# The causal mask of prompt attention: added by VectorE in PSUM in place of a bf16 product on TensorE

## Chip, cores and metric

The kernel runs on one core of one Trainium2 chip. The metric is device time in microseconds for one execution, lower is better. TensorE does matrix products and transposes into PSUM, VectorE and ScalarE read PSUM, GpSimd works on SBUF only, SyncE issues most of the DMAs.

## The reference

One step of a hybrid decoder layer: latent attention and a Mamba-2 scan in parallel, a gated merge, layer norm and a SwiGLU network, for a prompt of 1024 tokens and for 8 sequences with 4 new tokens each. Only the attention of the prompt matters here. Per head, of 16:

```python
def block(i):                       # 128 queries
    s = (einsum('bqhd,bkhd->bhqk', qn, k_nope)
         + einsum('bqhr,bkr->bhqk', qp, k_pe)).astype(float32) * ATTN_SCALE
    mask = key_pos[None, :] <= q_pos[:, None]
    s = where(mask, s, finfo(float32).min)
    p = softmax(s, axis=-1).astype(v.dtype)
    return einsum('bhqk,bkhd->bqhd', p, v)
```

A block of 128 queries with number q sees the (q + 1) * 128 keys up to its own end. Only the last 128 of these, the diagonal block, are cut by the mask.

## The kernel before

Each engine runs its own instruction list, written by hand, and semaphores order them. A stage of projections and of the scan comes first, then the prompt's attention (1218 to about 1530 us of the trace), then attention over the cached pages, then the branch products and the feed-forward network.

Attention handles two heads at a time, eight pairs in all. A pair's eight blocks of queries are split: G = 1 are the later four (q = 7 to 4, scores of 1024 to 640 keys), G = 0 the earlier four (q = 3 to 0, 512 to 128 keys). In each group the index i runs from 0 to 7: i % 2 is the head, i // 2 counts the blocks down from the longest. So there are 16 rows of scores in a pair, 128 in all.

PSUM has eight banks of 512 fp32. Head 0's scores are in banks 0 and 1, head 1's in banks 2 and 3. A row of G = 1 takes both banks of its head; rows of G = 0 take one, in turn. Bank 4 holds turned probabilities of head 0, bank 5 those of head 1, banks 6 and 7 the outputs.

For one row:

- TensorE (`scores`, L1155) multiplies the queries by the keys, 96 deep, in pieces of up to 512 keys. The product is fp32, and the trace shows two instructions for each piece. It waits for `s_read0` or `s_read1`, by which ScalarE says that the banks have been read.
- TensorE (L1157) adds the mask to the diagonal block: a bf16 identity `ident_b` times a bf16 table `after_b`, which holds 0 where a key is allowed and -1e30 where not. This product signals `s_ready`.
- VectorE (`row_max`, L2154) takes the row maximum from PSUM and scales it by a constant (L2156), which signals `m_ready`.
- ScalarE (`probs`, L1668) does the exponential with that maximum as bias, into SBUF (`pr`), with the row's sum beside it, and signals `s_read`.
- VectorE (`row_inverse`, L2161) takes the reciprocal of the sum of the row before; GpSimd (`scale_probs`, L805) multiplies the probabilities by it.
- TensorE turns the probabilities in tiles of 128x128 (`turn_probs`, L1169), head 0 then head 1. VectorE copies head 0's to SBUF (`turned`, L2166, `pt_read0`) and ScalarE head 1's (L1674). The next `turn_probs` waits for those copies.
- TensorE multiplies them by the values (`weigh`, L1179); ScalarE copies a finished output (`head_out`, L1679) and stores it.

The order on TensorE interleaves two groups. `later_rows` does the scores of G = 1 and turns and weighs the probabilities of G = 0; `earlier_rows` does the scores of G = 0 of the next pair and turns and weighs G = 1 of this one. VectorE's and ScalarE's lists follow the same order. Eight rows of G = 0 of the first pair stand ahead of all that. The inner pairs are a loop of two.

The tables `ident_b` and `after_b` are made by two casts on VectorE (L2133, L2134) at the end of the stage before; TensorE waits for them (`bf_ready`).

Of the kernel before, what the change touches and what calls it, by code (L numbers as in the profile page):

```python
# [9 lines left out]
BF16 = mybir.dt.bfloat16  # L10
I32 = mybir.dt.int32
ALU = mybir.AluOpType
# [3 lines left out]
P = 128  # L16
# [4 lines left out]
HEADS, NOPE, ROPE, VH = 16, 64, 32, 64  # L21
# [60 lines left out]
@contextmanager  # L82
def looped(eng, count, per):

    begun = {t: t.n for t in per}
    with eng.Fori(0, count) as i:
        for t, p in per.items():
            t.loops.append((i, p, t.n))
        yield i
    wrong = {t.sem.name: t.n - begun[t] for t, p in per.items() if t.n - begun[t] != p}  # L90
    assert not wrong, wrong
    for t, p in per.items():
        t.loops.pop()
        t.n += p * (count - 1)
# [57 lines left out]
def build(nc, a, o, stop=99, debug=None):  # L152
# [21 lines left out]
    def sem(name):  # L174
        if name in taken:
            return sem(taken[name][0])
        if name not in sems:
            sems[name] = nc.alloc_semaphore(name)
        return sems[name]
# [52 lines left out]
    def const(name):  # L232
        at, n = where[name]
        return cst[:, at:at + n]

    ident, ones = const("ident"), const("ones")
    V_GATE, V_QN, V_KVN, V_SSM, V_L1G, V_L1B, V_L2G, V_L2B, V_END = 0, 16, 19, 21, 37, 45, 53, 61, 69

    ps = nc.alloc_psum_tensor("ps", [P, 8, 512], F32)
# [30 lines left out]
    ar = Arena(floor)  # L270
# [5 lines left out]
    ar = Arena(floor)  # L276
# [20 lines left out]
    ar = Arena(floor)  # L297
# [9 lines left out]
    ar = Arena(at_conv)  # L307
# [24 lines left out]
    ar = Arena(at_z)  # L332
# [7 lines left out]
    ar = Arena(at_st)  # L340
# [3 lines left out]
    ar = Arena(at_cw)  # L344
# [3 lines left out]
    ar = Arena(at_cv)  # L348
# [3 lines left out]
    ar = Arena(at_so)  # L352
    s_new = [ar(f"s_new{b}", [P, 4, P]) for b in range(NEWS)]
    assert ar.at <= at_ccol
    ar = Arena(at_ccol)
    s_xe[1] = ar("s_xe1", [P, HG, SP_])
    assert ar.at <= at_crow
    ar = Arena(at_crow)
# [4 lines left out]
    ar = Arena(at_xo)  # L363
# [5 lines left out]
    ar = Arena(low)  # L369
# [24 lines left out]
    ar = Arena(at_kvt)  # L394
# [3 lines left out]
    ar = Arena(at_kvt)  # L398
    olat = ar("olat", [P, 2, HEADS, NS])
    oats = ar("oats", [P, HEADS // 2, NS])  # L400
    qb, kb, vb = [], [], []
    ar = Arena(low)
    for pp in range(2):
        qb.append([ar(f"qb{pp}{h}", [QH, SEQ]) for h in range(2)])
        kb.append([ar(f"kb{pp}{h}", [QH, SEQ]) for h in range(2)])
        if pp == 1:
            assert ar.at <= at_wkv
            ar = Arena(at_kvt)
        vb.append([ar(f"vb{pp}{h}", [P, SEQ // P, VH]) for h in range(2)])
    ident_b, after_b = ar("ident_b", [P, P], BF16), ar("after_b", [P, P], BF16)  # L410
    assert ar.at <= floor
    ar = Arena(at_g)
    pr = [[ar(f"pr{G}{i}", [P, (4 * G + 4 - i // 2) * P]) for i in range(8)] for G in range(2)]
# [5 lines left out]
    ar = Arena(low)  # L419
# [8 lines left out]
    ar = Arena(low)  # L428
# [399 lines left out]
    def _(pe):  # L828
        k = Counts()
        pe.wait_ge(sem("ident_full"), 16)  # L830

        for t in range(9):
# [4 lines left out]
            for j in range(KT):  # L837
                at = ps[:, 2 * b + j // 4, (j % 4) * n:(j % 4) * n + n] if n == P else ps[:, 2 * b, j * n:j * n + n]
# [161 lines left out]
        for j in range(DI // P):  # L1000
            last = pe.matmul(ps[:, 6, j * NS:(j + 1) * NS], spread[0:SH, j * P:(j + 1) * P], act_[:, SEQ:TOK],
                             start=True, stop=True)
# [137 lines left out]
            pe.wait_ge(sem(f"third_free{c}"), k[f"third_free{c}"].next())  # L1140
        pe.wait_ge(sem("xd_ready"), k["xd_ready"].next())
        pe.wait_ge(sem("kr_full"), k["kr_full"].next(64))
        pe.wait_ge(sem("bf_ready"), k["bf_ready"].next(2))

        def scores(pp, G, i):

            q, h, b = 4 * G + 3 - i // 2, i % 2, i % 2
            if G == 0 and i == 0:
                pe.wait_ge(sem(f"head_full{pp}"), k[f"head_full{pp}"].next(96))
            first_bank = 2 * b + (i // 2 % 2 if G == 0 else 0)  # L1150
            pe.wait_ge(sem(f"s_read{b}"), k[f"s_read{b}"].held() - (1 if G == 0 and i >= 2 else 0))
            length = (q + 1) * P
            for c in range(0, length, 512):
                w = min(512, length - c)
                pe.matmul(ps[:, first_bank + c // 512, 0:w], qb[pp][h][:, q * P:(q + 1) * P], kb[pp][h][:, c:c + w], start=True, stop=True)  # L1155
            at = q * P
            last = pe.matmul(ps[:, first_bank + at // 512, at % 512:at % 512 + P], ident_b[:, :], after_b[:, :], start=False, stop=True,  # L1157
                             skip_group_check=True)
            last.then_inc(sem("s_ready"), k["s_ready"].adds(1))

        def turn_probs(G, kb_):
# [689 lines left out]
    def _(dve):  # L1851
        k = Counts()
# [277 lines left out]

        dve.wait_ge(sem("unit_done"), 74)
        dve.tensor_copy(ident_b[:, :], ident).then_inc(sem("bf_ready"), k["bf_ready"].adds(1))  # L2133
        dve.tensor_copy(after_b[:, :], const("after")).then_inc(sem("bf_ready"), k["bf_ready"].adds(1))  # L2134

        def page_rows():
            dve.memset(krs[:, :], 0.0).then_inc(sem("pads_ready"), k["pads_ready"].adds(1))
# [10 lines left out]
        def row_max(G, i):  # L2148
            n = G * 8 + i
            length = (4 * G + 4 - i // 2) * P  # L2150
            first_bank = 2 * (i % 2) + (i // 2 % 2 if G == 0 else 0)
            src = ps[:, first_bank:first_bank + 2, :].rearrange("p a n -> p (a n)")[:, 0:length] if G else ps[:, first_bank, 0:length]
            dve.wait_ge(sem("s_ready"), k["s_ready"].next())
            dve.tensor_reduce(rowmax[:, n:n + 1], src, AX, ALU.max).then_inc(step.sem, step.adds(1))  # L2154
            dve.wait_ge(step.sem, step.same())
            dve.tensor_scalar(negmax[:, n:n + 1], rowmax[:, n:n + 1], -SCALE, None, ALU.mult).then_inc(sem("m_ready"), k["m_ready"].adds(1))  # L2156
# [29 lines left out]
                row_inverse(0, i - 1)  # L2186
        later_rows()
        page_rows()
        with looped(dve, HEADS // 4 - 1, {k["s_ready"]: 32, step: 32, k["m_ready"]: 32, k["inv_ready"]: 32, k["t_ready0"]: 24,
                                          k["pt_read0"]: 24} | pairs(k, {"s_read": 16})):  # L2190
            earlier_rows()
            later_rows()
            earlier_rows()
            later_rows()
# [313 lines left out]
```

## Time and profile before

| | us |
|---|---|
| median of 3 runs | 3173.14 |
| lowest and highest run | 3171.33, 3176.74 |
| profiled execution | 3172.03 |
| its span | 3170.2 |
| one pair of heads, from its first long score row to the next pair's | 37.45 |

The profile counts an engine as busy from an instruction's start to its end. A TensorE product's end is modelled and lies after the last column has gone in, so the ends of products overlap the next ones. What a product costs TensorE is read from start to start. Times within the trace count from the span's start.

### The profile page before, as it was taken

How to read it: one execution, taken by the hardware profiler on the slowest of the kernel's cores; microseconds unless marked ns; L12 is line 12 of the kernel's file. 1: busy time of each engine (PE TensorE's matmuls, PEld its weight loads, DVE VectorE, ACT ScalarE, POOL GpSimd, SP SyncE). 2: the span in 40 equal slices, each digit the busy share in tenths (PEclk: the TensorE clock that was granted, in tenths of full speed). 3: DMA queues.
4: the chain of work that ended last, by engine and by line, in shares of the span. 5: the costliest groups of instructions: out<-in, count | busy, mean ns of one | idle time of the engine just before them, and what ended most of it. 6: DMA issues, size and time to landing. Idle time of an engine off the chain costs nothing.

```text
span 3170.2 us, 46396 instructions
## 1 busy us (share of the span) xinstructions
PE 2978.9 (94%) x19012; PEld 2626.6 (83%) x19012; DVE 1558.7 (49%) x2120; ACT 756.7 (24%) x1151; POOL 1016.8 (32%) x546
## 2 busy tenths in 40 slices
PE   7889999999999999999999978999889999999996
PEld 7767999989998995555677668899789999999995
DVE  1661677774746464555344467665352222222226
ACT  1111121253535353545323110100120000000003
POOL 3331333332323322444211113344323333433330
PEclk9999999999999997999899989999999999999997
DMA  4134223555746445222343323353201111111101
GB/s 131 39 112 125 83 82 117 153 148 143 178 135 177 139 121 151 60 60 69 130 179 141 111 92 108 103 170 115 61 31 44 47 40 46 40 46 40 46 20 55
DMA packets 313405, 308.22 MB, mean 97 GB/s; under 512 B 31094, under 2 KB 271995, under 8 KB 310779
## 3 DMA queue, kind: packets, MB, share of 16 engines
q1 hardware_dynamic: 249768, 190.26, 21.3%
q10 hardware_dynamic: 59914, 78.22, 7.4%
q0 software_dynamic: 3584, 37.75, 3.1%
q8 instruction: 105, 1.72, 0.2%
q14 instruction: 34, 0.27, 0.0%
HBM read 227.97 MB, written 78.20 MB: 97 GB/s over the span
## 4 chain that ended last, share of the span: by engine, by line
PE 68%; DVE 12%; issue 9%; POOL 4%; DMA 3%; ACT 2%; SPq 1%; ACTq 0%; POOLq 0%; DVEq 0%
PE ps L859 41%; PE ps L1025 10%; POOL pr L805 4%; PE ps L1358 2%; PE ps L1301 2%; PE ps L1261 2%; PE ps L1274 2%; DVE cv L1956 2%; DVE flo L2445 1%; PE ps L1278 1%; PE ps L933 1%; PE ps L1104 1%; DVE cv L1950 1%; PE ps L1058 1%; DMA gt<-d_z 1%
## 5 line engine op out<-in xcount | busy, mean ns | idle before, releaser
L737 POOL TENSOR_TENSOR whi<-raw,cst 128x1024 fp32r<-128x1024 f32 x172 | 334.0, 1942 | 1404.9 <-PE ps L859 1273.1
L739 POOL TENSOR_TENSOR wlo<-raw,whi 128x1024 fp32r<-128x1024 f32 x172 | 469.5, 2730 | 13.5
L859 PE MATMUL ps<-ahi,whi 128*128 128x352 f32 x1824 | 400.2, 328 | 51.7 <-DVE alo L2316 21.5
L859 PE MATMUL ps<-alo,whi 128*128 128x352 f32 x1824 | 398.2, 327 | 0.0
L859 PE MATMUL ps<-ahi,wlo 128*128 128x352 f32 x1824 | 395.0, 325 | 0.0
L859 PEld LDWEIGHTS ps<-ahi,whi 128*128 128x128 f32 x1824 | 313.5, 191 | 58.7 <-issue 34.5
L859 PEld LDWEIGHTS ps<-ahi,wlo 128*128 128x128 f32 x1824 | 314.9, 190 | 0.0
L859 PEld LDWEIGHTS ps<-alo,whi 128*128 128x128 f32 x1824 | 313.6, 189 | 0.0
L1025 PE MATMUL ps<-xhi,whi 128*128 128x352 f32 x768 | 257.3, 335 | 0.6 <-ACT xraw L1534 0.4
L1025 PE MATMUL ps<-xlo,whi 128*128 128x352 f32 x768 | 248.8, 324 | 0.0
L1025 PE MATMUL ps<-xhi,wlo 128*128 128x352 f32 x768 | 248.8, 324 | 0.0
L2343 DVE TENSOR_TENSOR mm<-ps,mm 128x1056 f32<-128x1056 f32 x112 | 139.6, 1256 | 147.7 <-PE ps L859 146.3
L805 POOL TENSOR_TENSOR pr<-pr,rowinv 128x384 f32<-128x384 f32 (+7 forms) x128 | 145.5, 1146 | 202.5 <-DVE rowinv L2161 201.5
L1155 PE MATMUL ps<-kb,qb 96*128 96x512 f32 (+3 forms) x384 | 161.2, 538 | 10.8 <-ACT pr L1668 8.3
L859 PE MATMUL ps<-xhi,whi 128*128 128x352 f32 x720 | 158.4, 328 | 6.5 <-ACT xraw L1534 4.3
L859 PE MATMUL ps<-xlo,whi 128*128 128x352 f32 x720 | 157.3, 327 | 0.0
L859 PE MATMUL ps<-xhi,wlo 128*128 128x352 f32 x720 | 156.6, 326 | 0.0
L2154 DVE TENSOR_REDUCE rowmax<-ps 128x1 f32<-128x384 f32 (+7 forms) x128 | 96.9, 757 | 118.1 <-PE ps L1157 116.4
L1025 PEld LDWEIGHTS ps<-xhi,whi 128*128 128x128 f32 x768 | 145.3, 189 | 9.2 <-issue 6.8
L1155 PEld LDWEIGHTS ps<-kb,qb 96*128 96x128 f32 x384 | 65.5, 198 | 105.4 <-issue 76.9
L1025 PEld LDWEIGHTS ps<-xlo,whi 128*128 128x128 f32 x768 | 145.4, 189 | 0.0
L1025 PEld LDWEIGHTS ps<-xhi,wlo 128*128 128x128 f32 x768 | 145.2, 189 | 0.0
(320 smaller groups left out, 5015.8 us busy)
## 6 DMA issues: line engine op xcount, KB each, us to landing
raw<-in_w_in SPq DMA_DIRECT2D x61, 512.0 KB, 5.0
s_a<-d_acum SPq DMA_DIRECT2D x32, 512.0 KB, 7.1
d_xbc<-so ACTq DMA_DIRECT2D x24, 528.0 KB, 2.7
gt<-d_g SPq DMA_DIRECT2D x24, 528.0 KB, 3.7
raw<-in_w_ffn_gate SPq DMA_DIRECT2D x22, 512.0 KB, 3.7
raw<-in_w_ffn_up SPq DMA_DIRECT2D x22, 512.0 KB, 3.7
raw<-in_w_ffn_down SPq DMA_DIRECT2D x22, 512.0 KB, 3.5
d_z<-zo ACTq DMA_DIRECT2D x16, 528.0 KB, 5.0
```

Of the source, the lines that this page charges most:

```text
L737: pool.tensor_tensor(whi[s][:, :], raw[:, u], ones[:, 0:1].broadcast_to([P, UNIT]), ALU.mult).then_inc(sem("unit_hi"), k["unit_hi"].adds(1))
L739: pool.tensor_tensor(wlo[s][:, :], raw[:, u], whi[s][:, :].bitcast(F32), ALU.subtract).then_inc(sem("unit_split"), k["unit_split"].adds(1))
L805: pool.tensor_tensor(pr[G][i][:, :], pr[G][i][:, :], rowinv[:, n:n + 1].broadcast_to([P, length]), ALU.mult).then_inc(sem("n_ready"), k["n ...
L859: last = pe.matmul(ps[0:m, 3 * b + c, 0:width], w(j), x[:, j, at:at + width], start=i == 0, stop=i == n - 1)
L1025: last = pe.matmul(ps[:, c, 0:CH], w[u % SPLIT][:, j * P:(j + 1) * P], x[:, j, c * CH:(c + 1) * CH], start=i == 0, stop=i == 3 * KT - 1)
L1155: pe.matmul(ps[:, first_bank + c // 512, 0:w], qb[pp][h][:, q * P:(q + 1) * P], kb[pp][h][:, c:c + w], start=True, stop=True)
L1261: last = pe.transpose(ps[:, 4 + i % 3, r * P:(r + 1) * P], src, ident)
L1274: pe.matmul(half(c, s), qcur[b][:, j, :], kvt[:, j, 4 * g:4 * g + 4, :].rearrange("p r n -> p (r n)"), start=j == 0, stop=False)
L1301: last = pe.matmul(ps[64 * s:64 * s + 64, 7, 0:KL], prt[:, i, 64 * s:64 * s + 64], kvb[b][:, 8 * c + 4 * s + i % 4, :], start=i == 0, stop ...
L1358: last = pe.matmul(ps[:, 3 * b + c, 0:width], ones, src[:, at:at + width], start=start, stop=stop_)
L2154: dve.tensor_reduce(rowmax[:, n:n + 1], src, AX, ALU.max).then_inc(step.sem, step.adds(1))
L2343: dve.tensor_tensor(thirds(mm[:, e]), out3(b), thirds(mm[:, e]), ALU.add).then_inc(sem(f"res_free{b}"), k[f"res_free{b}"].adds(1))
```

## The change

The product L1157 goes, and so do the two bf16 tables, their casts and the wait for them. `s_ready` is now signalled by the last piece of the scores. VectorE gets a new first step in `row_max`: it adds the fp32 table `after`, which lies in SBUF already, to the diagonal 128 columns of the scores, reading and writing the same place in PSUM. The row maximum waits for this addition, on VectorE's own semaphore `dve_step`. The table in fp32 has the same values as the bf16 one.

```diff
-    ident_b, after_b = ar("ident_b", [P, P], BF16), ar("after_b", [P, P], BF16)
...
-        pe.wait_ge(sem("bf_ready"), k["bf_ready"].next(2))
...
                 w = min(512, length - c)
-                pe.matmul(ps[:, first_bank + c // 512, 0:w], qb[pp][h][:, q * P:(q + 1) * P], kb[pp][h][:, c:c + w], start=True, stop=True)
-            at = q * P
-            last = pe.matmul(ps[:, first_bank + at // 512, at % 512:at % 512 + P], ident_b[:, :], after_b[:, :], start=False, stop=True,
-                             skip_group_check=True)
+                last = pe.matmul(ps[:, first_bank + c // 512, 0:w], qb[pp][h][:, q * P:(q + 1) * P], kb[pp][h][:, c:c + w], start=True, stop=True)
             last.then_inc(sem("s_ready"), k["s_ready"].adds(1))
...
         dve.wait_ge(sem("unit_done"), 74)
-        dve.tensor_copy(ident_b[:, :], ident).then_inc(sem("bf_ready"), k["bf_ready"].adds(1))
-        dve.tensor_copy(after_b[:, :], const("after")).then_inc(sem("bf_ready"), k["bf_ready"].adds(1))
...
             dve.wait_ge(sem("s_ready"), k["s_ready"].next())
+            own = src[:, length - P:length]
+            dve.tensor_tensor(own, own, const("after"), ALU.add).then_inc(step.sem, step.adds(1))
+            dve.wait_ge(step.sem, step.same())
             dve.tensor_reduce(rowmax[:, n:n + 1], src, AX, ALU.max).then_inc(step.sem, step.adds(1))
...
-        with looped(dve, HEADS // 4 - 1, {k["s_ready"]: 32, step: 32, k["m_ready"]: 32, k["inv_ready"]: 32, k["t_ready0"]: 24,
+        with looped(dve, HEADS // 4 - 1, {k["s_ready"]: 32, step: 64, k["m_ready"]: 32, k["inv_ready"]: 32, k["t_ready0"]: 24,
```

No other instruction moves. VectorE's list shows it best in the earlier rows at i = 0 and 1, E0 and E1 in the prediction (`t_ready0` says that head 0's turned probabilities are in PSUM, `s_read` that a row's exponential is done). Before:

```order
L2154 TENSOR_REDUCE rowmax<-ps 128x1 [waits s_ready]
L2156 TENSOR_SCALAR negmax<-rowmax 128x1 [waits dve_step]
L2161 RECIPROCAL rowinv<-rowsum 128x1 [waits s_read1]
L2166 COPY ptb_213<-ps 128x128 [waits t_ready0]
L2154 TENSOR_REDUCE rowmax<-ps 128x1 [waits s_ready]
L2156 TENSOR_SCALAR negmax<-rowmax 128x1 [waits dve_step]
L2161 RECIPROCAL rowinv<-rowsum 128x1 [waits s_read0]
L2166 COPY ptb_211<-ps 128x256 [waits t_ready0]
```

With the change, the same place (the buffers' numbers differ, the buffers do not):

```order
L2151 TENSOR_REDUCE rowmax<-ps 128x1 [waits dve_step]
L2153 TENSOR_SCALAR negmax<-rowmax 128x1 [waits dve_step]
L2158 RECIPROCAL rowinv<-rowsum 128x1 [waits s_read1]
L2163 COPY ptb_211<-ps 128x128 [waits t_ready0]
L2149 TENSOR_TENSOR ps<-ps,cst 128x128 [waits s_ready]
L2151 TENSOR_REDUCE rowmax<-ps 128x1 [waits dve_step]
L2153 TENSOR_SCALAR negmax<-rowmax 128x1 [waits dve_step]
L2158 RECIPROCAL rowinv<-rowsum 128x1 [waits s_read0]
L2163 COPY ptb_209<-ps 128x256 [waits t_ready0]
```

The addition stands right behind the wait for the scores, ahead of the reciprocal and of the copy of the same step. Nothing changes places otherwise.

## Rows read from the trace of the kernel before

**Rows 1.** The page: busy time of the engines, share of the span, instructions
```profile
PE 2978.9 (94%) x19012; PEld 2626.6 (83%) x19012; DVE 1558.7 (49%) x2120; ACT 756.7 (24%) x1151; POOL 1016.8 (32%) x546
```

**Rows 2.** Busy time by stretches: stretch, length, busy us per engine, clock, DMA
```profile
1218.00:1240.00 22.00, 18.56 (x39) 8.74 (x40) 8.05 (x28) 7.44 (x20) 5.50 (x8) 0.54 0.56 169
...
1296.00:1332.00 36.00, 35.32 (x177) 18.28 (x175) 20.77 (x57) 17.79 (x43) 17.37 (x16) 1.00 0.20 59
```

**Rows 3.** The score line's products: min/median/max ns, first and last start, forms
```profile
L1155 PE MATMUL ps<-kb,qb x384: 272/592/1192, 1217.9 to 1515.1; 96*128 96x512 f32 x96, 96*128 96x384 f32 x32, 96*128 96x256 f32 x32, 96*128 96x128 f32 x32
```

**Rows 4.** Timeline: start us, us, engine, operation, count, idle before in brackets
```profile
1302.83 0.22 PE L1157 MATMUL ps<-after_b,ident_b 128*128 128x128 bf16 x1
...
1302.89 1.04 PE L1169 MATMUL ps<-cst,pr 128*128 128x128 f32 x8
1303.09 0.42 DVE L2154 TENSOR_REDUCE rowmax<-ps 128x1 f32<-128x256 f32 x1 [1.31 <-PE ps L1157]
1303.55 0.15 DVE L2156 TENSOR_SCALAR negmax<-rowmax 128x1 f32<-128x1 f32 x1
...
1309.60 1.98 PE L1155 MATMUL ps<-kb,qb 96*128 96x512 f32 x4
...
1347.05 1.98 PE L1155 MATMUL ps<-kb,qb 96*128 96x512 f32 x4
```

**Rows 5.** Timeline of rows L1 to L4 of the same pair
```profile
1314.14 0.19 ACT L1668 ACTIVATION_READ_ACCUMULATOR pr<-ps,negmax 128x1 f32 x1
...
1314.63 0.19 PEld L1155 LDWEIGHTS ps<-kb,qb 96*128 96x128 f32 x1 [0.33 <-ACT pr L1668]
...
1314.68 1.72 PE L1155 MATMUL ps<-kb,qb 96*128 96x512 f32 x4
...
1317.59 1.77 PE L1155 MATMUL ps<-kb,qb 96*128 96x512 f32 x4 [0.31 <-ACT pr L1668]
...
1318.63 1.01 ACT L1668 ACTIVATE pr<-ps,negmax 128x896 f32<-128x896 f32 x1 [0.60 <-ACT att L1679]
...
1319.78 1.56 PE L1155 MATMUL ps<-kb,qb 96*128 96x512 f32 x4 [0.36 <-ACT pr L1668]
```

**Rows 6.** Timeline of L6, E1 and E2 of that pair
```profile
1323.41 0.19 ACT L1668 ACTIVATION_READ_ACCUMULATOR pr<-ps,negmax 128x1 f32 x1
...
1324.02 1.30 PE L1155 MATMUL ps<-kb,qb 96*128 96x512 f32 x4
...
1330.16 0.19 ACT L1668 ACTIVATION_READ_ACCUMULATOR pr<-ps,negmax 128x1 f32 x1
...
1330.52 1.12 PE L1155 MATMUL ps<-kb,qb 96*128 96x512 f32 x2
...
1332.68 0.42 DVE L2166 COPY ptb<-ps 128x256 f32<-128x256 f32 x1
...
1333.20 0.42 PEld L1169 LDWEIGHTS ps<-cst,pr 128*128 128x128 f32 x4 [0.22 <-DVE ptb L2166]
...
1333.26 0.82 PE L1169 MATMUL ps<-cst,pr 128*128 128x128 f32 x6
```

**Rows 7.** Groups of VectorE: additions, or products, that read PSUM
```profile
L2097 DVE SCALAR_TENSOR_TENSOR s_new<-s_in,cdp,ps 128x128 f32<-128x128 f32 x128 | 35.9, 342 | 118.7 <-PE ps L1104 118.7
...
L2042 DVE TENSOR_TENSOR s_cb<-ps,cst 128x128 f32<-128x128 f32 x32 | 9.3, 289 | 46.9 <-ACT s_bt L1599 46.9
...
L2233 DVE TENSOR_TENSOR snew<-ps,cst 64x32 f32<-64x32 f32 x8 | 1.4, 172 | 0.0
```

**Rows 8.** Timeline of the start of the stage
```profile
1217.92 2.04 PE L1155 MATMUL ps<-kb,qb 96*128 96x512 f32 x2 [2.42 <-DVE after_b L2134]
...
1225.78 1.28 ACT L1668 ACT_TABLE_LOAD   x1 [15.00 <-DMA d_y<-s_y]
...
1231.66 0.27 DVE L2154 TENSOR_REDUCE rowmax<-ps 128x1 f32<-128x128 f32 x1
...
1232.10 3.75 PE L1155 MATMUL ps<-kb,qb 96*128 96x512 f32 x4 [0.52 <-ACT pr L1668]
```

## The prediction

> **What bounds the kernel now.** I read the page first. TensorE is busy for 94% of the span and VectorE for 49% [rows 1], so time taken from TensorE should count and time given to VectorE should be hidden. That is an average over stages, and the change touches one stage only: prompt attention, from 1218 to about 1530 us. The busy time by stretches says the same of it: TensorE 35.3 of 36 us, VectorE 20.8 of 36, clock 1.00 [rows 2]. So I went on to the order of events. VectorE's row maximum stood idle 1.31 us for the mask product at 1303.09 [rows 4]: VectorE, and ScalarE after it, hang on the product's end, with little queued before it. Last I read TensorE's own waits for softmax, in the timeline, for they tell whether a longer VectorE step is hidden.
>
> One pair of heads takes 37.45 us from its first score row to that of the next pair, 1309.60 to 1347.05 [rows 4]. There are eight pairs. I call the score rows of a pair L0 to L7 (rows of 1024 to 640 keys) and E0 to E7 (512 to 128 keys, of the next pair). Even numbers use one pair of banks, odd ones the other, so a score row waits until ScalarE's exponential of the row two before has read its banks. In this pair TensorE is already late at two rows: L3 starts 0.31 us and L4 0.36 us after TensorE fell idle, both released by the exponential [rows 5].
>
> **What is removed.** 128 mask products, 16 in a pair. The 0.22 us shown for one is not its price: TensorE is pipelined. The product starts at 1302.83 and the next transpose at 1302.89, so one costs 0.06 us of TensorE; the weight load lies under the row before [rows 4]. That is 0.96 us a pair and 7.7 us in all, if each counted. The end of a row is also signalled earlier, by 0.06 us: the product's start plus 0.22, against the last score product's stream end (the same moment) plus the 0.16 that a score product of 128 keys takes beyond its stream. That 0.16 is 0.27 us, the shortest score product, less 0.11 us, the step from one transpose of 128 columns to the next (eight take 1.04 us, the last 0.27 of it) [rows 3, 4].
> The two VectorE casts that made the bf16 tables go too. TensorE waited for the second until 1217.92, but ScalarE does its first exponential only after 1227.06, behind a wait for stores and a table load of 1.28 us [rows 8]; the first four rows fill the banks and then stand still for that. The 2.4 us so saved lie in this wait: worth nothing.
>
> **What is added.** 128 VectorE additions of 128x128 fp32, from PSUM and a constant into the same PSUM, plus a wait of the row maximum for it. No row of this trace has VectorE writing PSUM. The nearest row, PSUM and the constant table into SBUF at 128x128, is 289 ns. Below it stands a smaller one, 64x32, at 172; above it one with a third operand at 342 [rows 7]. I take 0.29 and keep 0.17 and 0.40 (the 342 with a margin of 60 ns for an unseen destination) as ends. The hand-over from one VectorE step to a dependent one is 0.035 us (row maximum from 1303.09 for 0.42, its scaling at 1303.55) [rows 4]. So each row's exponential comes 0.29 + 0.035 - 0.06 = 0.27 us later, counted from the end of its scores. On VectorE's queue the addition also stands ahead of the reciprocal for the row before and of the copy of turned probabilities.
> The Trainium skill (VectorE: DVE Perf Modes, The TRN2 errata) gives (N+151)/0.96 ns for an fp32 tensor_tensor, which is 291 ns here; its table of fixed costs gives 120 + N cycles from PSUM, 258 ns, by which the estimate would be about 1.2 us lower. The row's 289 ns agrees with the first. Its rules for authors say to minimise the count of chained VectorE operations, not the semaphores, which speaks against this change.
>
> **What of it is on the path, in one pair.** I go along TensorE and keep the lag behind the old schedule.
> - L0 and L1 run on without a wait. L1 starts 0.06 early.
> - L2 waits for L0's exponential. That was read out by 1314.33 and L2's weight load came at 1314.63. With 0.27 more and 0.05 for the semaphore the load comes at 1314.65 and the product 0.11 later, 1314.76 in place of 1314.68: lag 0.08.
> - L3 was already held by L1's exponential. L1 was 0.06 early and its exponential is 0.27 later: lag 0.21.
> - L4 is held through ScalarE's queue (a copy of the head's output and its store stand before L2's exponential): lag still 0.21 [rows 5].
> - L5 starts at 0.15. L6 waits for L4's exponential, read out by 1323.60, against a start at 1324.02. Add 0.21 and 0.27: 1324.08, plus 0.05 for the semaphore and 0.11 for the load, is 1324.24: lag 0.22.
> - E0 has no wait in this trace; the masks of L6 and L7 gone, the lag falls to about 0.1. E1 waits for L7's exponential, read out by 1330.35 (the read after it starts at 1330.16 and takes 0.19), against 1330.52. It gets L7's lag of 0.15 plus 0.27, so 1330.82 with the semaphore: lag 0.3 [rows 6].
> - E2's transposes wait for VectorE's copy at E1. It ended at 1333.10 and the transposes started at 1333.26: no slack, since 0.05 and 0.11 lie between. The copy now stands behind E1's addition: 0.3 + 0.27: lag 0.57 [rows 6]. The row of the weight load at 1333.20 names this copy as what ended its idle time.
> - From there nothing waits; the five masks of E3 to E7 give back 0.30.
> So a pair ends 0.27 us later, with about 1.5 us of new or longer waiting and 0.96 of product gone, less what the old waits swallowed. Seven such pairs: 1.9 us. Four additions of the 16 stand in the chain.
>
> **The start.** Before the first pair, eight rows of short scores run at clock 0.54 [rows 2], and the tail of it is VectorE and ScalarE turn by turn: the last maximum starts at 1231.66, each waiting behind the reciprocal of the row before, then L0 at 1232.10 when the seventh row's is out [rows 8]. Five additions (third to seventh row), 5 x 0.325 = 1.6, less 0.2 where ScalarE and not VectorE set the pace: 1.4 us, with no TensorE time to give back. The first long rows at half clock: 0.3. The last pair reaches L7's addition, whose exponential frees the gather of cached pages: 0.1 us. Sum: 1.4 + 1.9 + 0.3 + 0.1 = 3.7 us.
> The profiled execution takes 3172.03 us, 1.8 more than its span and 1.1 less than the median of 3173.14. I put the 3.7 on the median: **3176.8 us**, 0.12% slower, which is within 0.2% (6.3 us), about what a measurement of this kernel can tell from no change.
>
> **Its bounds.** In the sum, 0.01 us of addition is worth 28 x 0.01 in the pairs and about 9 x 0.01 at the start and the end, 0.37 us. An addition of 0.17 gives -0.7 us, 0.22 no change, 0.34 gives +5.5, 0.36 the mark of 6.3, 0.40 gives +7.8. The clock is still low in the first stretch; if it rises 3 us earlier or later than before, that moves about 1 us. With the spread of the three runs, 5.4 us, this makes 3171 to 3184.
>
> **Rivals.**
> 1. *The addition into PSUM is dear* (slower by over 0.2%). Reading and writing PSUM in one operation has no row. From 0.36 us on the time passes the mark; at 0.45 the four chained additions cost 0.9 us a pair and the total is about +9.6: 3182.7. For it: no row shows the destination, and the three-operand row has 342. Against: the fixed parts of the copy, maximum and addition rows from PSUM lie close together. 0.23.
> 2. *The products were free already.* If the next fp32 load only moves into the place of the mask's hidden load, the 0.06 isn't given back and the pair ends 0.8 us later in all, not 0.27: 7 x 0.8 + 1.8 = 7.4, 3180.5. Against: transposes with the same kind of load follow each other at 0.11 us, just their streaming [rows 4]. 0.05.
> 3. *VectorE hides it all* (faster). The chain at L3, E1 and E2 would have to have slack; then 0.96 a pair comes back less 1.4 at the start: -5.3, and at most -7.7: 3165.4 to 3167.8. For it: VectorE idles 15 us of 36. Against: the three waits above. Faster by over the mark: 0.05.
> 4. *The clock.* New waits of 0.3 us lower the granted clock once a pair: taken as 3 us at half speed, 1.5 us lost, eight times: +12 on top, 3189. The Trainium skill (TensorE: Matmul & The Clock Gate, Part 1) ties the clock to recent activity. In this stage the clock stays at 1.00 with waits of 0.3 to 0.4 us present [rows 2, 5]. 0.02.
> My own case has 0.65.
>
> **Chances.** Some of my case's upper end and rival 2 pass the mark, some of rival 3 stays below it: faster 0.05, within 0.2% 0.66, slower 0.29.
>
> **What would show it.** The addition's row near 290 ns, 128 times; the pair's period up by about 0.27 from 37.45; TensorE's wait at E1 and at E2's transposes new, about 0.3 each; L3's idle time 0.2 longer and L4's unchanged; L0 of the first pair 1.4 us later; transposes starting 0.06 earlier after their score row; everything behind the stage shifted alike. The forecast fails if the addition takes over 0.36, if E1 and E2 show no wait, or if the clock in the stage leaves 1.00.

## The result: 0.74% slower, outside the range

| | us, median | lowest to highest | runs |
|---|---|---|---|
| before | 3172.74 | 3169.39 to 3176.74 | 6 |
| with the change | 3196.32 | 3192.36 to 3197.48 | 6 |

The ratio is 1.0074, interval 1.0061 to 1.0086: 23.6 us slower, where 3.7 had been forecast and 3184 was the upper end. The changed kernel's profiled execution took 3196.32 us at a span of 3194.5, against 3170.2 in the trace of before.

First its page: the engines' busy time, and the two queues that bring instructions (packets, MB, share of the DMA engines). Before, the page has 105 packets and 1.72 MB on q8, and 34 and 0.27 on q14.

```profile
PE 2985.0 (93%) x18884; PEld 2628.0 (82%) x18884; DVE 1594.8 (50%) x2246; ACT 757.0 (24%) x1151; POOL 1019.3 (32%) x546
...
q8 instruction: 140, 2.29, 0.3%
q14 instruction: 44, 0.36, 0.0%
```

Against [rows 1] TensorE has 128 products less, as the change says, yet its busy time grew by 6 us. It ran slower somewhere. And 45 more packets of instructions came in, 35 on q8 and 10 on q14, though the kernel has fewer instructions on TensorE. Neither was in the prediction.

The addition itself came out as forecast (line L2149: shortest/median/longest in ns, then what ended VectorE's idle time ahead of it, in us and times):

```profile
L2149 DVE TENSOR_TENSOR ps<-ps,cst x128: 278/300/300, 1218.9 to 1535.0; 128x128 f32<-128x128 f32 x128
its engine sat idle before it (us, times) until:
  PE ps L1154: 84.3, 92
  issue: 9.7, 5
```

The last line is the odd one. "Issue" is idle time that no semaphore explains, and 9.7 us of it in five places is much. The timeline has two of them, of 4.71 and 4.06 us. This is the first (VectorE, then TensorE, ScalarE and the weight load, which wait for it), then VectorE's rows of the second:

```profile
1334.79 0.17 DVE L2158 RECIPROCAL rowinv<-rowsum 128x1 f32<-128x1 f32 x1
...
1335.83 1.12 PE L1154 MATMUL ps<-kb,qb 96*128 96x512 f32 x2
1339.66 0.30 DVE L2149 TENSOR_TENSOR ps<-ps,cst 128x128 f32<-128x128 f32 x1 [4.71 <-issue]
...
1340.91 0.69 ACT L1664 ACTIVATE pr<-ps,negmax 128x512 f32<-128x512 f32 x1 [4.98 <-DVE negmax L2153]
...
1341.29 0.71 PEld L1165 LDWEIGHTS ps<-cst,pr 128*128 128x128 f32 x4 [5.16 <-DVE ptb L2163]
1341.29 1.12 PE L1165 MATMUL ps<-cst,pr 128*128 128x128 f32 x4 [4.34 <-DVE ptb L2163]
```

```profile
1417.00 0.16 DVE L2158 RECIPROCAL rowinv<-rowsum 128x1 f32<-128x1 f32 x1
1421.22 0.30 DVE L2149 TENSOR_TENSOR ps<-ps,cst 128x128 f32<-128x128 f32 x1 [4.06 <-issue]
```

E0's scores were being computed and VectorE did nothing. Between the reciprocal and the addition its list holds only the end of the loop over heads and the jump back to its start. In the 16 us around it, 1330 to 1346, q14 brought four packets:

```profile
q14 instruction: 4, 0.03, 0.6%
```

In the trace of before the same place (line L2154 is the row maximum there), where q14 brought none, reads:

```profile
1329.92 0.69 DVE L2154 TENSOR_REDUCE rowmax<-ps 128x1 f32<-128x512 f32 x1 [0.38 <-issue]
```

Busy time by stretches (columns as in [rows 2]) shows what TensorE's clock did. The last line is 8 us right behind the first standstill.

```profile
1296.00:1332.00 36.00, 34.66 (x164) 17.34 (x162) 25.06 (x73) 17.60 (x43) 16.58 (x16) 1.00 0.24 67
1332.00:1368.00 36.00, 31.02 (x134) 15.57 (x133) 20.47 (x62) 14.03 (x36) 11.92 (x13) 0.91 0.22 59
1368.00:1404.00 36.00, 35.23 (x164) 17.67 (x162) 24.77 (x73) 17.51 (x44) 16.59 (x17) 1.00 0.24 66
...
1341.00:1349.00 8.00, 7.71 (x32) 4.71 (x34) 4.30 (x14) 3.43 (x10) 3.33 (x3) 0.61 0.09 34
```

TensorE waited 4.34 us, and then ran at 1.2 in place of 2.4 GHz for 8 x 0.39 / 0.5 = 6.2 us of these 8, which costs 3.1 more. So one standstill costs about 7 us.

I cut both traces at the same events. All numbers are us:

| stretch | before | after | difference |
|---|---|---|---|
| up to ScalarE's first exponential of the attention | 1227.1 | 1227.5 | +0.4 |
| from there to L0 of the first pair | 5.04 | 6.25 | +1.2 |
| first pair, L0 to L0 | 40.03 | 43.21 | +3.2 |
| third and fifth pair | 37.45, 37.46 | 44.56, 44.14 | +13.8 |
| second, fourth, sixth, seventh | 37.47, 37.45, 37.45, 37.45 | 37.67, 37.64, 37.65, 37.71 | +0.8 |
| last pair, to its L7 | 17.2 | 17.3 | +0.1 |
| from there to the feed-forward's loop | 986.2 | 985.6 | -0.6 |
| the feed-forward's loop, four periods | 580.0 | 587.8 | +7.8 |
| the rest | 89.9 | 87.4 | -2.5 |

The last pair's end to the loop took 981 to 989 us, and the rest 87 to 91, in the traces of all kernels below with no order in it, so these two lines are left out of the account. Each line is from one execution of each kernel.

### The profile page after: what moved, and what is told of

The parts are those of the page before. It is cut to its first block, busy times and chain, and to the rows that moved or that the text cites. A ratio compares the mean times of both kernels' runs of the same rounds, so it can differ in the third digit from the quotient of the medians.

```text
span 3194.5 us, 46362 instructions
## 1 busy us (share of the span) xinstructions
PE 2985.0 (93%) x18884; PEld 2628.0 (82%) x18884; DVE 1594.8 (50%) x2246; ACT 757.0 (24%) x1151; POOL 1019.3 (32%) x546
## 4 chain that ended last, share of the span: by engine, by line
PE 65%; DVE 14%; issue 10%; POOL 5%; DMA 3%; ACT 2%; SPq 0%; ACTq 0%; POOLq 0%; DVEq 0%
PE ps L859 39%; PE ps L1025 10%; POOL pr L805 4%; DVE cv L1952 2%; PE ps L1354 2%; PE ps L1297 2%; PE ps L1257 2%; PE ps L1270 2%; DVE flo L2442 1%; PE ps L1274 1%; PE ps L933 1%; DVE cv L1946 1%; PE ps L1104 1%; PE ps L1058 1%; PE ps L1062 1%
## 5 line engine op out<-in xcount | busy, mean ns | idle before, releaser
L859 PE MATMUL ps<-fhi,whi 128*128 128x352 f32 x528 | 117.4, 331 | 22.0 <-DVE mm L2340 22.0
```

Of the source, the lines that this page charges most:

```text
L859: last = pe.matmul(ps[0:m, 3 * b + c, 0:width], w(j), x[:, j, at:at + width], start=i == 0, stop=i == n - 1)
```

## The experiments

The theory to test: **a longer loop body on VectorE has to be fetched anew at each jump back, and TensorE's list, shorter by 128 instructions ahead of its feed-forward loop, makes that loop fetch as well.** The rival: the addition itself, through its waits, through PSUM or through the clock. Each kernel of a series ran beside the kernel before, whose medians there were 3169.82, 3172.75 and 3173.13.

**a_unroll.** The changed kernel, with VectorE's loop written out, so that there is no jump. No operation differs.

```diff
-        with looped(dve, HEADS // 4 - 1, {k["s_ready"]: 32, step: 64, ...}):
+        for _ in range(HEADS // 4 - 1):
```

> The changed kernel with VectorE's loop over pairs of attention written out (three bodies in a row, no jump back); TensorE's and ScalarE's loops stay. Theory code: the two idle times of VectorE of 4.7 and 4.1 us at its jumps back are instruction fetch, since its loop body grew by 64 instructions; without a jump they vanish, the two long pairs fall from 44.56 and 44.14 us to about 37.7, the granted clock stays at 1.00 there, and the kernel is 13 us faster than the change: about +10 us against the kernel before. Rival work: the idle time belongs to the addition and its waits themselves; then the pairs stay at 44 us and the kernel at +23.6 us.

Measured: 3182.68 us, ratio 1.0041 (1.0022 to 1.0060). The third and fifth pair take 37.56 us in place of 44.56 and 44.14. The standstills and the low clock behind them are gone, with every addition still there. That rules out the addition as their cause. VectorE's rows at the place of the first jump:

```profile
1336.44 0.27 DVE L2163 COPY ptb<-ps 128x128 f32<-128x128 f32 x1
1337.41 0.30 DVE L2149 TENSOR_TENSOR ps<-ps,cst 128x128 f32<-128x128 f32 x1 [0.70 <-PE ps L1154]
```

The list still has to be fetched: from 1324 to 1516 us q14 brought four packets, one in about 64 us. But where there is no jump this cost nothing that the trace shows. Between the first and the last of them VectorE ran 386 instructions, or 129 to a packet, so a block of 8 KB holds 128 of them. q8 stayed at 140 packets and the feed-forward's four periods at 589.2 us.

**a_pages.** The changed kernel with the four small steps that turn page numbers into indices moved, on VectorE's list, from ahead of the first E0 to ahead of the attention's last group of rows.

```diff
         def page_rows():
             dve.memset(krs[:, :], 0.0)...
             dve.memset(kts[:, :], 0.0)...
+        def page_index():
             dve.wait_ge(sem("pages_full"), ...)
...
         later_rows()
+        page_index()
         earlier_rows(False)
```

> The changed kernel with VectorE's four small steps on the page indices moved from ahead of the second group of the first pair to just ahead of the last pair's end. Theory clock: these steps and the addition together make TensorE wait 1.66 us there, and the clock falls to 1.2 GHz for the next microseconds; moved, the first pair takes about 40.3 us in place of 43.2 and the kernel is 3 us faster than the change, about +20.5. Rival: the first pair is long because of the start of the stage; then it stays at 43 us.

Measured: 3193.62 us, ratio 1.0073 (1.0054 to 1.0092). In the whole time that can't be told from the changed kernel, but the first pair fell from 43.21 to 38.81 us. In the changed kernel these rows stand there:

```profile
1255.31 1.13 DVE L2134 CAST pgf<-pgi 128x8 f32<-128x8 int32 x1
...
1257.13 0.30 DVE L2149 TENSOR_TENSOR ps<-ps,cst 128x128 f32<-128x128 f32 x1
...
1258.77 1.11 PE L1165 MATMUL ps<-cst,pr 128*128 128x128 f32 x4 [1.66 <-DVE ptb L2163]
```

Before, TensorE's wait at this place was 1.16 us and the clock behind it stayed high:

```profile
1256.56 0.66 PE L1169 MATMUL ps<-cst,pr 128*128 128x128 f32 x4 [1.16 <-DVE ptb L2166]
```

With the addition on top it is 1.66, and the clock falls (stretches of the changed kernel, then of before):

```profile
1258.00:1266.00 8.00, 7.23 (x27) 4.29 (x28) 3.99 (x15) 3.37 (x9) 3.33 (x3) 0.57 0.85 185
```

```profile
1257.00:1265.00 8.00, 8.00 (x51) 4.53 (x49) 4.67 (x16) 4.82 (x13) 4.28 (x5) 1.00 0.67 157
```

So of the 3.2 us of the first pair 0.5 are the longer wait, and the rest is the half clock that it set off. a_pages has 0.27 us of wait there and a clock of 1.00.

**b_dvepad and a_pepad.** Both were to add empty instructions, but those never reached the program, and neither trace has a record of one: each is a repeat of the kernel that it was made from.

> The kernel before (mask by the product, no addition) with two empty VectorE instructions behind each row's scaled maximum: its loop body grows by 64 instructions, as in the change, with no work added. Theory code: VectorE stands idle 4 to 5 us at each of the two jumps back, those pairs take some 6.5 us more, and the kernel is 13 to 15 us slower than before. Rival work: only the instructions' own time, 32 times some 0.05 us a pair off the path: within 2 us of before.

> The changed kernel with 129 empty instructions on TensorE, put where it waits for ScalarE's first exponential, so that all later TensorE code lies where it lay before the change. Theory code position: the 4 to 5 us that the changed kernel loses in the feed-forward loop (35 more instruction packets there) come from the loop's code lying over one block more; the packets fall from 140 to about 105 and the kernel is 4 us faster than the change, about +19.5 us against before. Rival: the drift in the feed-forward loop is chance of one profiled execution; then nothing changes, +23.6 us.

Measured: 3167.68 us, ratio 0.9992 (0.9980 to 1.0003), and 3198.32 us, ratio 1.0090 (1.0068 to 1.0112). As repeats they say how firm the pattern is. The second again has long third and fifth pairs (44.17 and 45.64), a first of 42.03 and 140 packets on q8; the first has none of it.

**b_dvepad2.** The kernel before, product kept, with two one-column memsets more in each row of VectorE. Its loop body has as many instructions as that of the changed kernel, 291 in place of 227 (the traces hold as many VectorE records from one jump to the next).

```diff
+            for j in range(2):
+                dve.memset(pads[:, 2 * n + j:2 * n + j + 1], 0.0)
```

> The kernel before, with two real but idle VectorE instructions (a memset of one column of a spare tile) behind each row's scaled maximum: VectorE's loop body grows by 64 instructions as in the change, with no addition and no new wait of anyone. (The empty instructions of the run with the same aim never reached the program.) Theory code: VectorE stands idle 4 to 5 us at each of its two jumps back and those two pairs take 43 to 45 us; with the rest the kernel is 13 to 15 us slower than before. Rival work: the idle time comes with the additions; then the pairs stay near 37.5 us and the kernel within 2 us of before.

Measured: 3173.23 us, ratio 1.0003 (0.9990 to 1.0015). All pairs but the first take 37.45 to 37.47. The theory in its plain form, that 291 instructions are too many, falls. VectorE at the jump, and its queue:

```profile
1335.96 0.16 DVE L2164 RECIPROCAL rowinv<-rowsum 128x1 f32<-128x1 f32 x1
...
1336.52 0.69 DVE L2155 TENSOR_REDUCE rowmax<-ps 128x1 f32<-128x512 f32 x1 [0.40 <-issue]
```

```profile
q14 instruction: 34, 0.28, 0.0%
```

What differs is where the body lies. Counted from the start of VectorE's list in the program, and in blocks of 128 (q14's packets are 0.27 MB / 34 = 8 KB):

| kernel | loop, instructions | in blocks | blocks touched | standstills |
|---|---|---|---|---|
| before | 1002 to 1229 | 7.83 to 9.60 | 3 | none |
| with the change | 1016 to 1307 | 7.94 to 10.21 | 4 | 4.71, 4.06 us |
| b_dvepad2 | 1034 to 1325 | 8.08 to 10.35 | 3 | none |

That gave the new form: the body must not touch a fourth block. It can be tested both ways by moving a loop without changing it. Where the edges of the blocks lie is not seen in a trace: a count that begins up to 7 instructions earlier or 10 later would sort all the kernels here in the same way.

**a_shift.** The changed kernel with 18 memsets ahead of the attention's first row.

```diff
+        for j in range(18):
+            dve.memset(pads[:, 32 + j:33 + j], 0.0)
         for i in range(8):
             row_max(0, i)
```

> The changed kernel with 18 one-column memsets on VectorE ahead of its first row of prompt attention. Nothing in the loop of heads changes: its body stays 291 instructions, but it now begins at instruction 1034 of VectorE's program in place of 1016. Position theory (the jump back costs nothing while the body lies in three blocks of 128 instructions, 8 KB, and VectorE stands when it lies in four: 1016 to 1307 touches blocks 7 to 10, 1034 to 1325 blocks 8 to 10): no standstill at 1342 and 1424, all pairs from the second on 37.6 to 37.7 us, 44 or so transfers on queue 14 become 34 to 38, and the time falls by the 6.9 and 6.5 us of the two long pairs to about 3183 (3180 to 3186). Size theory (64 more instructions in the body are too many wherever they lie): pairs of 44 us stay, 3196. The feed-forward's fetches for TensorE stay by both.

Measured: 3185.15 us, ratio 1.0046 (1.0031 to 1.0060). Third and fifth pair 37.68 and 37.64. Its VectorE at the first jump, and its queue:

```profile
1337.05 0.16 DVE L2159 RECIPROCAL rowinv<-rowsum 128x1 f32<-128x1 f32 x1
1337.61 0.30 DVE L2150 TENSOR_TENSOR ps<-ps,cst 128x128 f32<-128x128 f32 x1 [0.40 <-issue]
```

```profile
q14 instruction: 35, 0.29, 0.0%
```

Eighteen instructions more made the kernel 11 us faster than the changed one (3196.32), at the upper end of what had been expected.

**b_shift.** b_dvepad2 with 110 memsets ahead of the first row: loop at 1144 to 1435, 8.94 to 11.21, four blocks.

> The kernel before, its product kept, with two memsets more in each row (body 291 instructions, as in b_dvepad2, which showed no standstill with the loop at 1034 to 1325) and 110 one-column memsets ahead of the first row, so that the loop lies at 1144 to 1435, blocks 8 to 11. Position theory: VectorE stands about 4 to 5 us at each of the first two jumps back and TensorE drops to half clock for some us after: two pairs of 43 to 45 us where before all had 37.45; with up to 6 us for the 110 memsets, 3186 to 3193. Size theory, or theory that only the addition's own instructions do it: no standstill, pairs 37.45, 3172 to 3180.

Measured: 3188.38 us, ratio 1.0059 (1.0045 to 1.0074). Pairs of 45.13 and 43.30 us where b_dvepad2 had 37.45, in a kernel that has no addition at all, behind standstills of 3.91 and 4.92 us. The first:

```profile
1330.28 0.07 DVE L2159 MEMSET pads<- 128x1 f32 x2
1334.35 0.69 DVE L2155 TENSOR_REDUCE rowmax<-ps 128x1 f32<-128x512 f32 x1 [3.91 <-issue]
```

```profile
q14 instruction: 46, 0.37, 0.0%
```

Both signs came out as the position theory has them, and 1144 is just 128 past the 1016 of the changed kernel, while 1034 between them is free of it: the pattern came back after 128 instructions. That settles that place and not size decides on VectorE.

One more thing is in this trace. b_shift changes nothing on TensorE, yet q8 has 114 packets where before has 105. All nine are in the first of the four feed-forward periods (2511 to 2660 us):

```profile
q8 instruction: 9, 0.15, 0.4%
```

That period took 148.5 us from jump to jump, the others 144.2 to 145.8; before, the same four took 145.8, 144.2, 145.8 and 144.2. So the loop can fetch in its old place too, and the period that does is 2.7 us longer within the same execution.

**a_pepad2 and b_pepad126.** These are on TensorE's list. 64 one-column products added to the changed kernel at the attention's start put its feed-forward loop back to within one instruction (the wait for the casts, which is gone) of its old place; 63 added to the kernel before push it out by 126, for each product comes with a weight load. Both edits also put the last four of the first eight score rows behind four waits.

```diff
+        for _ in range(64):
+            pe.matmul(ps[0:32, 4, 0:1], ident.bitcast(BF16)[:, 0:32], ident.bitcast(BF16)[:, 0:1], start=True, stop=True)
```

> The changed kernel with 64 tiny bf16 products on TensorE (one column each into bank 4, read by nobody) where it waits for ScalarE's first exponential: TensorE's code behind them lies where it lay before the change. Theory code position: the feed-forward loop no longer fetches instructions, the packets fall from 140 to about 105, and the kernel is 5 to 8 us faster than the change (about +16 us against before), with attention still long at the two jumps. Rival: the feed-forward loop's drift is chance; then +23.6 us.

> The kernel before with 63 such tiny products at that place. Its TensorE code behind them lies 126 instructions later; the change had moved it 128 or 129 earlier, which is nearly the same place within a block of 256. Theory code position: the feed-forward loop now fetches as in the change (about 140 packets) and the kernel is 5 to 8 us slower than before with attention untouched. Rival: no fetches, within 2 us of before; or the size and not the place counts.

Measured: 3197.29 us, ratio 1.0088 (1.0062 to 1.0113), and 3178.86 us, ratio 1.0023 (1.0012 to 1.0034). The second is clear: with nothing changed behind the attention's first rows, q8 brings 9 packets in each of the four feed-forward periods where before it brings none, and these go from 580.0 to 589.4 us, with all pairs but the first still at 37.45 to 37.47. The first failed to repair it: 27 packets, in three of the four periods, and 590.6 us.

**a_clean.** The changed kernel with a_unroll, a_pages and the 64 products together.

> The changed kernel with all three repairs: VectorE's loop of pairs written out, the 64 tiny TensorE products, and the page index steps moved to the last pair. What is left is the trade of the product for the addition, as the prediction summed it: first pair about 39 us, further pairs 37.55, about +2 to +5 us against the kernel before. If something else of the change costs time, it stays at +8 or more.

Measured: 3172.62 us, ratio 1.0009 (0.9993 to 1.0025). First pair 38.74, others 37.56 to 37.63. With the side effects mostly gone, the trade of product for addition can't be told from no change. TensorE's program is that of a_pepad2, yet q8 brought 18 packets here, in two periods (585.7 us in all). Together with b_shift: at the old place, or one instruction off it, a period is fetched in some executions and not in others. In five traces at the old place it was one period of 20, one instruction off 5 of 8. Whether that one instruction matters isn't shown.

**a_final.** The changed kernel with its loop kept and moved (24 memsets), the page steps moved, and 70 products, which put the feed-forward loop 11 or 12 instructions past its old place.

> The changed kernel with its loops kept and three repairs: 24 memsets on VectorE ahead of the first row (loop at 1036 to 1327, three blocks), the page index steps behind the attention, and 70 one-column products on TensorE at the attention's start (its feed-forward loop then begins at 20662, against 20650 before and 20522 in the changed kernel). Position theory: no standstill of VectorE, all pairs 37.6 to 37.7, first pair 38.8; in the feed-forward queue 8 brings 1 block in place of 37 and its four loop periods come to 580 us in place of 588; attention costs 298.6 us against 296.2 before, so 2.5 more, partly hidden later: 3172 to 3176, within 0.1% of the kernel before. If the feed-forward's fetches have nothing to do with the position: 37 blocks again, 586 to 590 us, 3178 to 3182.

Measured: 3177.23 us, ratio 1.0021 (1.0011 to 1.0032). That is above the 3172 to 3176 expected, and 3.5 to 10 us above the kernel before. Inside the one trace, of an execution of 3175.81 us, every part came out: L0 rows 38.7 and 37.7 us apart,

```profile
1239.89 2.07 PE L1155 MATMUL ps<-kb,qb 96*128 96x512 f32 x2 [1.59 <-ACT pr L1669]
...
1278.61 1.99 PE L1155 MATMUL ps<-kb,qb 96*128 96x512 f32 x4
...
1316.27 1.98 PE L1155 MATMUL ps<-kb,qb 96*128 96x512 f32 x4
...
1353.92 1.55 PE L1155 MATMUL ps<-kb,qb 96*128 96x512 f32 x3
```

105 packets on q8 as before, and four periods of 580.1 us. TensorE's waits in the feed-forward's loop (for what, us in total, times, longest) in the changed kernel, then in a_final:

```profile
PE ps L859 <- DVE mm L2340: 17.4, 8, 2.2
PE ps L859 <- issue: 3.4, 4, 1.2
```

```profile
PE ps L860 <- DVE mm L2350: 17.0, 8, 2.2
```

One of these issue waits, from the last product before the loop's jump to the first behind it:

```profile
2668.66 0.65 PE L859 MATMUL ps<-fhi,wlo 128*128 128x352 f32 x3
2670.46 0.75 PE L859 MATMUL ps<-ahi,whi 128*128 128x352 f32 x3 [1.16 <-issue]
```

The waits are 3.4 of the 7.8 us; 4.0 more is busy time of TensorE (567.1 us in the four periods against 563.1), and most of that is the clock. Here is the same place of the second period, 60 us behind its jump, in the changed kernel and in the one before:

```profile
2726.20:2729.60 3.40, 3.40 (x13) 3.40 (x12) 0.13 (x1) 0.00 (x0) 0.00 (x0) 0.50 0.00 0
```

```profile
2706.00:2709.40 3.40, 3.40 (x23) 3.40 (x23) 1.26 (x1) 0.00 (x0) 0.00 (x0) 1.00 0.00 0
```

The changed kernel has such a stretch of 3.4 us at half clock in each of its four periods, before and a_final in two of the four. A period with one has 1.5 us more busy time (141.5 against 140.0), so two more are 3.0 of the 7.8 us, and the fetches with their waits are the other 4.8, 1.2 a period. Over all traces there are one or two such stretches where no period is fetched and four or five where all four are. Why the clock falls there, tens of microseconds behind the wait, stays open.

**b_pages.** The kernel before with the page steps moved, as the partner of a_final.

> The kernel before with the page index steps on VectorE moved behind the attention, nothing else. If they cost the first pair its long wait on the VectorE copy, the pair goes from 40.0 to about 38.6 us and the time to 3171.3; if the half clock later or the wait is set otherwise, 40.0 stays and the time is 3172.7.

Measured: 3171.58 us, ratio 1.0003 (0.9991 to 1.0015): no difference in the whole time; in the trace the first pair takes 38.31 in place of 40.03. From the first exponential to the last L7 it has 285.3 us and a_final 288.1. So **the trade itself costs 2.8 us in its stage**: 1.1 at the start, 0.4 in the first pair, 1.1 in the six others, and 0.1 at the end. a_final's time is more than that above both b_pages and before (medians, by 5.7 and 4.1 us); no trace shows where the difference lies, and a_final has its 24 memsets and 70 products besides. No kernel here is measurably faster than the one before.

## Why the prediction was wrong

Its sum for the operations held; a cost outside the sum was six times as large. By its own steps:

- *The addition*: taken as 0.29, measured 0.30 us. Its rival 1, addition into PSUM dear from 0.36 on, did not come. The row of 289 ns was the right neighbour, and the addition with its destination in PSUM takes 11 ns more than that row. A small slip in the bounds: by its own 0.37 us for 10 ns an addition of 0.22 gives 1.1 us, not "no change".
- *What is on the path, in one pair.* In the undisturbed fourth pair of the changed kernel, L0, L3, L4, E1, E2's transposes and the next L0:

```profile
1359.18 1.98 PE L1154 MATMUL ps<-kb,qb 96*128 96x512 f32 x4
...
1367.38 1.77 PE L1154 MATMUL ps<-kb,qb 96*128 96x512 f32 x4 [0.56 <-ACT pr L1664]
1369.57 1.56 PE L1154 MATMUL ps<-kb,qb 96*128 96x512 f32 x4 [0.42 <-ACT pr L1664]
...
1380.38 1.13 PE L1154 MATMUL ps<-kb,qb 96*128 96x512 f32 x2 [0.27 <-ACT pr L1664]
...
1383.29 0.64 PEld L1165 LDWEIGHTS ps<-cst,pr 128*128 128x128 f32 x6 [0.69 <-DVE ptb L2163]
...
1396.82 1.12 PE L1154 MATMUL ps<-kb,qb 96*128 96x512 f32 x2
```

  Counted from L0 to the product's start and set against [rows 4 to 6], L3 is 0.21 late (forecast 0.21), L4 0.21 (0.21), E1 0.28 (0.3), E2's transposes 0.45 (0.57) and the next L0 0.19 (0.27). E1's wait and the longer one for the copy are there. The walk was right to 0.12 us. (Its 0.05 for the semaphore and 0.11 for the load are 0.10 and 0.06 in the copy's row; only their sum enters.) Six pairs at 0.2 and the first at 0.4 to 0.5 make 1.7 where 1.9 was forecast.
- *The start*: 1.2 us from the first exponential to L0, forecast 1.4 ([rows 8] against the exponential at 1227.50 and L0 at 1233.74 in the changed kernel).
- *The products*: rival 2, that they cost nothing, would have shown as 0.8 us a pair. It did not come.
The first cost 2.7 us: without the page steps ahead of E0 the pair is 4.4 us shorter with the addition (a_pages) and 1.7 shorter without it (b_pages). What failed here is that the pair walked was a regular one, and the first, with a page cast ahead of E0, where TensorE already waited 1.16 us, got no walk of its own; the sum has only 0.3 for its first rows.
- The prediction named the sign of its own failure, the clock in the stage leaving 1.00, but no mechanism that would bring it.

Together: 1.2 + 0.5 + 1.2 + 0.1 for the trade is 3.0 (forecast 3.7), 2.7 for the clock in the first pair, 13.4 for VectorE's jumps and 7.8 for TensorE's make 26.9, against a difference of spans of 24.3; the -2.6 between lie in the stretches that scatter (+0.4, -0.6 and -2.5 in the table).

The Trainium skill has this rule (Runtime: NRT & Kernel Launch, Instruction fetch mechanics): a taken branch whose target is outside the window of code that the engine holds has to fetch it, and the engine stands until it is there. The runs agree with it, at 3.9 to 4.9 us for VectorE. The page has the window as two blocks of 16 KiB. By that, with any start of the count, the changed kernel and b_shift, which lie 128 instructions apart, could not both touch three such blocks; both stood, so on VectorE the measured rule, three blocks of 8 KB pass and four do not, is the one to go by here. With this rule the prediction would have had a rival at about 3172.7 + 3.7 + 2 x 7 = 3190.

## What to carry to other kernels

A kernel with loops in its instruction lists has a cost that no dependency shows: count, for each engine and each loop, how many blocks of code the body touches before and after an edit, for loops far behind the edit too, and look at the profile's instruction queues (34 against 44 packets on one and 105 against 140 on the other told it here). In a trace, a long idle stretch at a loop's jump with "issue" as its end, and packets on the instruction queue beside it, point to this; 0.4 us was there without any fetch. A few cheap instructions ahead of the loop may mend it: 18 memsets gave back 11 us. And walk the irregular pair, not only the regular one: there 0.5 us more of waiting was followed by a half clock that cost 2.7.

## What was not expected of the hardware

- VectorE stood 3.9 to 4.9 us at a jump back when its loop of 291 instructions lay at 1016 or 1144 of its list (four blocks of 8 KB by that count), and 0.4 us, no more than with 227, when it lay at 1034 or 1036 (three).
- The same list with the loop written out fetched a block in about 64 us and never stood for it.
- TensorE's loop of about 1770 instructions, with its jump, is fetched as 9 packets of 16 KB in a period or not at all. Moved by 126 to 129 instructions either way it fetched in every period (588 to 590 us for four), 11 or 12 past its old place in none (580 us). At the old place it fetched in one period of 20 and one instruction off in 5 of 8.
- What the granted clock did behind a wait was not the same each time. In the first pair waits of 1.16 to 1.19 us left it at 1.00 in five traces. Waits of 1.44 and 1.66 us were followed by 3.4 to 6.8 us at 1.2 GHz, waits of 3.05 to 4.34 us at the standstills by 3.4 to 10.2 us.
- An fp32 addition of 128x128 that reads and writes PSUM takes 300 ns, against 289 with SBUF as the destination.
